# Shift and scale of the dense stage: from VectorE's sums to TensorE's two lines, inside the attention

## The chip, the cores and the metric

The kernel runs on one core of one Trainium2 chip. The metric is device time in microseconds (us), the median of several executions. TensorE is called PE in the profile, VectorE DVE, ScalarE ACT, GpSimd POOL, SyncE SP.

## The reference

Two blocks of two layers each, over 256 tokens of width 1024. The first block has a hybrid mixer (gated linear attention beside a sparse attention with a compressed, a selected and a window branch), a dense feed-forward part, a Mamba-2 mixer and a mixture of experts. Ahead of each of the four stands a modulation that depends on the conditioning vector `c` alone:

```python
def adaln(c, w, b):
    mod = jax.nn.silu(c) @ w + b
    shift, scale, gate = jnp.split(mod[:, None, :], 3, axis=-1)
    return shift, scale, gate

def modulate(x, norm_w, shift, scale):
    return rmsnorm(x, norm_w) * (1 + scale) + shift
```

`w` is 1024 x 3072 in float32, so each of shift (part 0), scale (part 1) and gate (part 2) is a vector of 1024 numbers out of 4 MB of weights. The change is about how shift and scale of the dense stage are computed, and when.

## The kernel before

The stages of the first block follow one another: hybrid input projection with the gated linear attention, the sparse attention, the hybrid output projection with the residual addition and norm, the dense stage, then Mamba and experts. Each engine has its own program, in an order written out by hand; semaphores tie them. Weights of 2 MB a piece come over SyncE's queue into `slots`.

The modulation vectors that are not needed at once are made beside this main work, and called side work here. `SIDE` lists it: the gate of hyb, then dense, ssm and moe, each with its parts. A part is eight chunks `k` of 128 rows by 1024 columns, 512 KB each, loaded by GpSimd into three buffers in turn: `beside[0]`, `beside[1]` and a `gates` buffer. VectorE multiplies chunk `k` by `sc[:, k]` (silu of c, one number a partition) and adds it to the accumulator `macc` (128 x 1024): line 150 for the first chunk, line 153 for the others. After the eighth chunk the sum over the 128 partitions is left, and TensorE makes it. For shift and scale these are eight products with a column of ones (`column_sums`), and `column_done` adds the bias and writes `s2` or `s1` (in the trace `s_dense`, `s_ssm`). For the gate, which is needed on all partitions, they are two products of 128x512 with a matrix of ones, each followed on VectorE by the addition of the bias rows (`gate`); the one side bank of the attention is taken by them in turn. A buffer is loaded again when its accumulation has signalled; `macc` can be started again when the sums are made.

Three generators hold this side work for GpSimd, VectorE and TensorE (`side_gpsimd`, `side_vector`, `side_tensor`). The main programs advance them by one unit wherever `c.side_v.step()` or `c.side_t.step()` stands; `pace = (a, b)` lets through those of every b calls that the test in `step` allows, and `until` runs the side work up to a named point. Only these calls set where a side instruction stands in an engine's order. An instruction whose data are late holds up all that stands behind it on its engine.

In the sparse attention `branch_*` are the selected and the window branch (scores `S<-..`, their transposes by `k_ident`, products `vb,PT`), `compressed_*` makes the compressed keys (`xk`, hidden `hx`, `hy`, `hz`, its transpose `hid`, then `kcT` and `vbd`), and `blocks_*` scores them (`cs`, `cp`, `ct`, `AT`). Its output is `mix`, which the output projection takes.

Of the kernel before, what the change touches and what calls it, by code (L numbers as in the profile page):

```python
# [437 lines left out]
SIDE = (("hyb", 0, 2, (2,)), ("dense", 1, 2, (0, 1, 2)), ("ssm", 2, 2, (0, 1, 2)), ("moe", 0, 0, (0, 1, 2)))  # L438
# [316 lines left out]
def first(c):  # L755
# [105 lines left out]

    def column_done(e, tsig, vsig, name, part):
# [65 lines left out]
    def jobs():  # L928
        for name, slot, third, which in SIDE:
            chunks = [(p, k) for p in which for k in range(KC)]  # L930
            yield name, slot, [beside[:, 0, :], beside[:, 1, :], gates[third][:, :]], chunks

    def side_gpsimd(e, me):

        free = [S.t.at(("cols", now[-1])), NOTHING, S.t.at(("mod", "hyb", 1))]
        for name, slot, bufs, chunks in jobs():
# [4 lines left out]
            def get(n):  # L941
                part, k = chunks[n]
                e.wait_ge(*free[n % 3])
                e.dma_start(bufs[n % 3], w[k * 128:(k + 1) * 128, part * D:(part + 1) * D]).then_inc(*beside_landed[n % 3].up((name, n)))
# [5 lines left out]
            for n, (part, k) in enumerate(chunks):  # L950
# [3 lines left out]
                free[n % 3] = side.v.at((name, n))  # L954
# [13 lines left out]
    def side_vector(e, me):  # L968
        last = NOTHING
        for name, slot, bufs, chunks in jobs():  # L970
            yield
            yield
            for n, (part, k) in enumerate(chunks):
                yield
                e.wait_ge(*beside_landed[n % 3].at((name, n)))
                if k == 0:
                    e.wait_ge(*last)
                    e.tensor_scalar(macc[:, :], bufs[n % 3], sc[:, 0:1], ALU.mult).then_inc(*side.v.up((name, n)))
                else:
                    e.wait_ge(*side.v.at((name, n - 1)))  # L980
                    e.scalar_tensor_tensor(macc[:, :], bufs[n % 3], sc[:, k:k + 1], macc[:, :], ALU.mult, ALU.add).then_inc(*side.v.up((name, n)))
# [4 lines left out]
                yield  # L986
                yield
# [15 lines left out]
    def side_tensor(e, me):  # L1003
        for name, slot, bufs, chunks in jobs():
            yield
            yield
            for n, (part, k) in enumerate(chunks):
                yield
                if k < KC - 1:
                    continue  # L1010
# [3 lines left out]
                yield  # L1014
                if part < 2:
                    column_sums(e, side.t, macc, side.v.at((name, n)), name, part, c.side_banks)
                    me.done.add((name, ("cols", part)))
                    continue
                for i in range(2):
                    ps = c.side_banks.take(("gate", name, i))  # L1020
                    e.wait_ge(*ps.was)
                    e.wait_ge(*side.v.at((name, n)))
# [10 lines left out]
def hybrid(c):  # L1033
# [400 lines left out]
    def compressed_tensor(e):  # L1434
# [13 lines left out]
        c.side_t.step()  # L1448
        for _ in range(3):
            yield  # L1450
# [37 lines left out]
    def compressed_vector(e):  # L1488
# [23 lines left out]
        c.side_v.step()  # L1512
        for _ in range(3):
            yield
# [31 lines left out]
    def blocks_tensor(e, hf):  # L1546
        qs = slice(hf * 128, hf * 128 + 128)
        for gi in range(2):
# [6 lines left out]
            m.then_inc(*t.up(("Sc", hf, gi)))  # L1555
            yield
# [3 lines left out]
        e.transpose(ps.t[:, 0:128], small[hf][4][:, :], K["ident"]).then_inc(*t.up(("pc", hf)))  # L1560
        yield
# [4 lines left out]
        e.matmul(ps.t[:, :], small[hf][5][:, :], vbd[:, :, :].rearrange("p a d -> p (a d)")).then_inc(*t.up(("oc", hf)))  # L1566
        yield
# [10 lines left out]
    def blocks_vector(e, hf):  # L1578
# [3 lines left out]
        for gi in range(2):  # L1582
# [6 lines left out]
            if gi == 0:  # L1589
                yield  # L1590
        mine = v.now()
        yield
# [18 lines left out]
        c.psum.leave(("nsa_pc", hf), v)  # L1611
        yield
# [4 lines left out]
        c.psum.leave(("nsa_oc", hf), v)  # L1617
        yield

    def branch_tensor(e, br):  # L1620
# [3 lines left out]
        for hf in range(2):  # L1624
# [3 lines left out]
            for gi in range(2):  # L1628
                for j0 in range(0, 4, per):
# [4 lines left out]
                    m.then_inc(*t.up(("s", br, hf, gi, j0)))  # L1634
                yield
# [19 lines left out]
            m.then_inc(*t.up(("o", br, hf)))  # L1655
            yield
# [23 lines left out]
    def branch_vector(e, br):  # L1680
# [3 lines left out]
        for hf in range(2):  # L1684
            nk = (hf + 1) * 128
            per = 512 // nk
            for gi in range(2):
# [10 lines left out]
                e.tensor_reduce(mx_[:, gi * 4:gi * 4 + 4], S_[:, gi * 4:gi * 4 + 4, 0:nk], ALU.max, negate=True).then_inc(*v.up(("max", br, hf, gi)))  # L1698
                yield
# [19 lines left out]
            c.psum.leave(("nsa_o", br, hf), v)  # L1719
            yield  # L1720
# [25 lines left out]
    def tensor(e):  # L1746
        c.side_banks = bs
        e.wait_ge(*v.at(("HT", 7)))
# [6 lines left out]
        S.t.mark("in_end")  # L1755
# [2084 lines left out]
```

## Time and profile before

| | |
|---|---|
| time, median of 3 | 2633.59 us (2630.77 to 2640.56) |
| profiled execution | 2639.54 us, its span 2637.7 us |
| busy share of TensorE, VectorE, ScalarE, GpSimd | 92%, 75%, 54%, 8% |
| input projection (45.3 to 156.0) | 110.7 us |
| sparse attention (156.0 to 264.4) | 108.4 us |
| output projection, residual, norm (264.4 to 304.4) | 40.0 us |
| dense stage (304.4 to about 516.8) | 212.4 us |

The stages lie one behind the other, so a stage's time is that of the chain through it. The busy shares are means over stages that are bound in different ways. Times inside the trace are from the start of the span.

### The profile page before, as it was taken

The numbers are of one execution on the slowest core, as the hardware profiler recorded it, in microseconds if no ns is written. First come the engines' busy times: TensorE is split into PE (matmuls) and PEld (weight loads), VectorE is DVE, ScalarE is ACT, GpSimd is POOL, SyncE is SP. The second block draws the span as 40 slices with busy tenths as digits, with TensorE's granted clock in tenths as the row PEclk, the third lists the DMA queues.
The fourth block names the chain that finished last, engine by engine and source line by source line (L and its number), as shares of the span: only waits on it lengthen the run. The fifth ranks groups of instructions, "written<-read, shape, count | busy, mean of one in ns | idle before, by whom it ended". The sixth has DMA issues, their size and how long they took to land.

```text
span 2637.7 us, 32879 instructions
## 1 busy us (share of the span) xinstructions
PE 2425.0 (92%) x13850; PEld 2105.0 (80%) x13850; DVE 1984.6 (75%) x2208; ACT 1431.5 (54%) x1594; POOL 210.9 (8%) x265
## 2 busy tenths in 40 slices
PE   4877899898899999999999999998997999897998
PEld 3756799687777888888888888887886997886997
DVE  6756777686657888989888889886666775767675
ACT  3312443464546777767676767675444653444562
POOL 1101001000000000000000000000311110221110
PEclk8986899897889999999999999999998999998999
DMA  9652678432246999999999999995224453323551
GB/s 317 214 201 88 213 273 297 161 133 92 96 171 231 348 361 347 360 349 359 352 354 345 360 342 365 340 368 186 96 76 151 162 211 136 115 78 118 197 185 76
DMA packets 263559, 608.44 MB, mean 231 GB/s; under 512 B 18472, under 2 KB 33083, under 8 KB 263403
## 3 DMA queue, kind: packets, MB, share of 16 engines
q1 hardware_dynamic: 247808, 554.39, 58.4%
q0 software_dynamic: 14640, 51.49, 5.7%
q8 instruction: 111, 1.82, 0.3%
q10 hardware_dynamic: 954, 0.37, 0.1%
q14 instruction: 46, 0.37, 0.0%
HBM read 605.17 MB, written 1.05 MB: 230 GB/s over the span
## 4 chain that ended last, share of the span: by engine, by line
PE 80%; DVE 10%; ACT 5%; DMA 2%; issue 1%; POOL 1%; SPq 0%; PEldq 0%; PEld 0%; DVEq 0%; ACTq 0%; POOLq 0%
PE ps L132 78%; PE ps L136 2%; DVE eb L153 1%; DMA slots<-in_hyb_mod_w 1%; DVE X L153 1%; ACT L142 1%; DVE ul_in L145 1%; DVE xn L153 1%; DVE macc L153 1%; ACT uh_ffn L139 0%; DMA beside<-in_dense_mod_w 0%; ACT eb L139 0%; ACT xn L139 0%; DVE ul_ssm_w L145 0%; DVE gate L153 0%
## 5 line engine op out<-in xcount | busy, mean ns | idle before, releaser
L145 DVE TENSOR_TENSOR ul_moe_w<-slots,uh_moe_w 128x2048 fp32r<-128x2048 f32 x334 | 762.6, 2290 | 108.4 <-ACT uh_moe_w L139 108.2
L139 ACT ACTIVATE uh_moe_w<-slots 128x2048 fp32r<-128x2048 f32 x334 | 640.1, 1918 | 215.7 <-PE ps L132 188.9
L132 PE MATMUL ps<-uh_moe_w,XGh 128*128 128x512 f32 x896 | 356.6, 398 | 3.1 <-DVE XGl L145 2.1
L132 PE MATMUL ps<-uh_moe_w,XGl 128*128 128x512 f32 x896 | 349.5, 390 | 0.0
L132 PE MATMUL ps<-ul_moe_w,XGh 128*128 128x512 f32 x896 | 348.9, 389 | 0.0
L145 DVE TENSOR_TENSOR ul_ffn<-slots,uh_ffn 128x2048 fp32r<-128x2048 f32 x62 | 142.1, 2292 | 100.7 <-ACT uh_ffn L139 100.7
L132 PE MATMUL ps<-HTf,uh_ffn 128*128 128x256 f32 x704 | 201.2, 286 | 2.8 <-DVE HTlf L145 2.8
L132 PE MATMUL ps<-HTf,ul_ffn 128*128 128x256 f32 x704 | 200.8, 285 | 0.0
L132 PE MATMUL ps<-HTlf,uh_ffn 128*128 128x256 f32 x704 | 200.8, 285 | 0.0
L132 PEld LDWEIGHTS ps<-uh_moe_w,XGh 128*128 128x128 f32 x896 | 168.3, 188 | 38.8 <-DVE XGl L145 2.3
L132 PEld LDWEIGHTS ps<-uh_moe_w,XGl 128*128 128x128 f32 x896 | 168.2, 188 | 35.8
L132 PEld LDWEIGHTS ps<-ul_moe_w,XGh 128*128 128x128 f32 x896 | 168.4, 188 | 35.1 <-issue 1.7
L139 ACT ACTIVATE uh_ffn<-slots 128x2048 fp32r<-128x2048 f32 x66 | 125.7, 1911 | 96.1 <-PE ps L132 96.1
L132 PE MATMUL ps<-uh_moe_w,ehTh 128*128 128x512 f32 x448 | 177.2, 395 | 0.0
L132 PE MATMUL ps<-ul_moe_w,ehTh 128*128 128x512 f32 x448 | 174.6, 390 | 0.0
L132 PEld LDWEIGHTS ps<-HTf,uh_ffn 128*128 128x128 f32 x704 | 137.0, 195 | 3.6 <-DVE HTlf L145 3.6
L132 PE MATMUL ps<-uh_moe_w,ehTl 128*128 128x512 f32 x448 | 138.1, 389 | 0.0
L132 PEld LDWEIGHTS ps<-HTlf,uh_ffn 128*128 128x128 f32 x704 | 136.9, 194 | 0.0
L132 PEld LDWEIGHTS ps<-HTf,ul_ffn 128*128 128x128 f32 x704 | 136.8, 194 | 0.0
L145 DVE TENSOR_TENSOR ul_dense_w<-slots,uh_dense_w 128x2048 fp32r<-128x2048 f32 x33 | 75.5, 2291 | 45.0 <-ACT uh_dense_w L139 45.0
L145 DVE TENSOR_TENSOR ul_ssm_w<-slots,uh_ssm_w 128x1024 fp32r<-128x1024 f32 (+1 forms) x57 | 68.5, 1204 | 54.0 <-ACT uh_ssm_w L139 53.9
L132 PE MATMUL ps<-HTm,uh_in 128*128 128x256 f32 (+1 forms) x336 | 102.5, 305 | 7.2 <-DVE HTlm L145 4.1
(511 smaller groups left out, 5565.0 us busy)
## 6 DMA issues: line engine op xcount, KB each, us to landing
slots<-in_moe_w_gu SPq DMA_DIRECT2D x111, 2048.0 KB, 8.6
slots<-in_moe_w_down SPq DMA_DIRECT2D x56, 2048.0 KB, 8.1
slots<-in_w_up SPq DMA_DIRECT2D x20, 2048.0 KB, 7.9
slots<-in_w_in SPq DMA_DIRECT2D x14, 2048.0 KB, 8.5
slots<-in_dense_w_gu SPq DMA_DIRECT2D x10, 2048.0 KB, 10.1
slots<-in_ssm_w_in SPq DMA_DIRECT2D x10, 2048.0 KB, 8.1
slots<-in_w_down SPq DMA_DIRECT2D x10, 2048.0 KB, 8.4
slots<-in_dense_w_down SPq DMA_DIRECT2D x5, 2048.0 KB, 12.3
```

Of the source, the lines that this page charges most:

```text
L132: return self.e.matmul(o, lhsT, rhs, start=start, stop=stop, skip_group_check=skip) if self.e else DONE
L136: return self.e.transpose(o, i, ident[0:n, 0:n]) if self.e else DONE
L139: return self.e.activation(o, i, f, **kw) if self.e else DONE
L142: return self.e.preload_act_table_set("natural_log_exp_and_others") if self.e else DONE
L145: return self.e.tensor_tensor(o, a, b, op) if self.e else DONE
L153: return self.e.scalar_tensor_tensor(o, a, s, b, op0, op1) if self.e else DONE
```

## The change

Dense part 2 (the gate) is now made first, by VectorE as before. Parts 0 and 1 follow it inside the attention, and TensorE makes them without VectorE's accumulation: for each chunk two products, the column `sc[:, k]` of 128 partitions as weights against each half of the chunk, accumulated over the eight chunks. They end in two lines of 512 numbers, on partitions 0 and 64 of one PSUM bank. VectorE copies the two lines to partition 0 of `macc`, and eight products of one row each turn them into the eight columns that `column_done` expects. A buffer of these two parts is freed by TensorE's products.

With this the steps move: a pace of (3, 5) in the input projection, one of (1, 1) in the attention with more places for steps, and `until` at both ends of the attention. The orders of ScalarE and SyncE stay as they were.

```diff
-SIDE = (("hyb", 0, 2, (2,)), ("dense", 1, 2, (0, 1, 2)), ("ssm", 2, 2, (0, 1, 2)), ("moe", 0, 0, (0, 1, 2)))
+SIDE = (("hyb", 0, 2, (2,)), ("dense", 1, 2, (2,)), ("dense", 1, 2, (0, 1)), ("ssm", 2, 2, (0, 1, 2)), ("moe", 0, 0, (0, 1, 2)))
+LINES = (("dense", (0, 1)),)
...
+    def lines_tensor(e, name, part, k, x, landed):
+
+        if k == 0:
+            ps = c.side_banks.take(("lines", name, part))
+            e.wait_ge(*ps.was)
+        ps = c.psum.of(("lines", name, part))
+        e.wait_ge(*S.v.at("sc"))
+        e.wait_ge(*landed.at((name, part, k)))
+        for i, r in enumerate((0, 64)):
+            m = e.matmul(ps.t[r:r + 1, :], sc[:, k:k + 1], x[:, i * 512:(i + 1) * 512], k == 0, k == KC - 1)
+        m.then_inc(*side.t.up((name, part, k)))
+
+    def lines_to_columns(e, name, part):
+
+        ps = c.side_banks.take(("mod", name, part))
+        e.wait_ge(*ps.was)
+        e.wait_ge(*S.g.at("ones"))
+        e.wait_ge(*side.v.at(("lines", name, part)))
+        for i in range(8):
+            m = e.matmul(ps.t[:, i:i + 1], macc[0:1, i * 128:(i + 1) * 128], ones[0:1, 0:1])
+        m.then_inc(*side.t.up(("mod", name, part)))
...
     def side_gpsimd(e, me):
...
-                free[n % 3] = side.v.at((name, n))
+                free[n % 3] = (side.t if by_lines else side.v).at((name, part, k))
...
     def side_vector(e, me):
...
+                if by_lines:
+                    ps = c.psum.of(("lines", name, part))
+                    e.wait_ge(*side.t.at((name, part, k)))
+                    e.wait_ge(*last)
+                    for i, r in enumerate((0, 64)):
+                        e.tensor_copy(macc[0:1, i * 512:(i + 1) * 512], ps.t[r:r + 1, :]).then_inc(*side.v.up(("lines", name, part)))
+                    c.psum.leave(("lines", name, part), side.v)
...
     def side_tensor(e, me):
...
+                if by_lines:
+                    lines_tensor(e, name, part, k, bufs[n % 3], beside_landed[n % 3])
...
     def tensor(e):
         c.side_banks = bs
+        c.side_t.pace = (3, 5)
...
         S.t.mark("in_end")
+        c.side_t.until(("hyb", "rows"))
+        c.side_t.pace = (1, 1)
         weave(branch_tensor(e, 0), branch_tensor(e, 1), blocks(e, 0, compressed_tensor, blocks_tensor), blocks(e, 1, None, blocks_tensor))
+        c.side_t.until(("dense", ("cols", 1)))
```

VectorE's program (`vector`) gets the same four lines for `c.side_v`. A `step()` is added in the loops of `branch_tensor` and `branch_vector` (behind the scores and behind the products), in `blocks_tensor` and `blocks_vector` (behind each piece), and in the three waiting turns of `compressed_tensor` and `compressed_vector`.

TensorE's order in the middle of the attention, from the last chunk products of part 0 to the scores of the second half. A product is named out<-moving,weights; `hx` is the hidden layer of the compressed keys, `vb,PT` the branches' output products, `kb,nq` the scores:

```order
+L132 MATMUL ps<-beside,sc 1x512 x2
+L136 MATMUL ps<-k_ident,S 128x128 x2
+L132 MATMUL ps<-beside,sc 1x512 x2
 L136 MATMUL ps<-k_ident,hx 128x30 x4
 L132 MATMUL ps<-vb,PT 128x64 x16
+L132 MATMUL ps<-ones,macc 128x1 x8
 L132 MATMUL ps<-hid,w 64x16 x4
-L132 MATMUL ps<-kb,nq 128x256 x8
+L132 MATMUL ps<-kb,nq 128x256 x4
+L132 MATMUL ps<-gate,sc 1x512 x2
+L132 MATMUL ps<-kb,nq 128x256 x4
+L132 MATMUL ps<-beside,sc 1x512 x2
```

The chunk products (1x512) now stand ahead of the transposes of `hx`, and the eight products that make the columns of part 0 ahead of the work with `hid`, all in front of `kb,nq`.

VectorE's order at the same place, from the hidden layer's last operations to the first scores of the second half:

```order
 L145 TENSOR_TENSOR hx<-hx,hz 30x512
-L153 SCALAR_TENSOR_TENSOR macc<-gate,sc,macc 128x1024
-L153 SCALAR_TENSOR_TENSOR macc<-beside,sc,macc 128x1024 x2
-L156 COPY PT<-ps 128x2x128
-L153 SCALAR_TENSOR_TENSOR macc<-gate,sc,macc 128x1024
-L156 COPY PT<-ps 128x2x128
-L153 SCALAR_TENSOR_TENSOR macc<-beside,sc,macc 128x1024 x2
-L153 SCALAR_TENSOR_TENSOR macc<-gate,sc,macc 128x1024
+L156 COPY PT<-ps 128x2x128 x2
 L156 COPY hid<-ps 128x4x15 x2
 L145 TENSOR_TENSOR Og<-ps,fac 128x512
+L156 COPY macc<-ps 1x512 x2
 L145 TENSOR_TENSOR mix<-ps,fac 128x512
+L145 TENSOR_TENSOR s_dense<-ps,v_m 128x8
```

Seven accumulations are gone from between `hx` and `hid`; the copy of the two lines and `s_dense` stand behind `hid`.

VectorE's order at the end of the attention, up to `mix`, where before the copies of PT, `AT`, `Og` and `mix` had three accumulations of ssm among them:

```order
 L153 SCALAR_TENSOR_TENSOR macc<-gate,sc,macc 128x1024
+L156 COPY PT<-ps 128x512
+L153 SCALAR_TENSOR_TENSOR macc<-beside,sc,macc 128x1024
+L145 TENSOR_TENSOR AT<-ps,cf 128x512
+L153 SCALAR_TENSOR_TENSOR macc<-beside,sc,macc 128x1024
+L145 TENSOR_TENSOR AT<-ps,cf 128x512
+L153 SCALAR_TENSOR_TENSOR macc<-gate,sc,macc 128x1024
+L153 SCALAR_TENSOR_TENSOR macc<-beside,sc,macc 128x1024 x2
 L145 TENSOR_TENSOR Og<-ps,fac 128x512
 L145 TENSOR_TENSOR mix<-ps,fac 128x512
+L145 TENSOR_TENSOR s_ssm<-ps,v_m 128x8
 L145 TENSOR_TENSOR mix<-mix,AT 128x512 x2
```

Here accumulations of ssm part 0 have been moved in, and with them its column (`s_ssm`), which stands ahead of the two additions that finish `mix`. On GpSimd the loads of two more chunks (`beside<-in_ssm_mod_w`) stand ahead of the `AT` additions.

## Rows read from the trace of the kernel before

**Rows 1.** The page: span, and TensorE's busy time and share

```profile
span 2637.7 us, 32879 instructions
...
PE 2425.0 (92%) x13850; PEld 2105.0 (80%) x13850; DVE 1984.6 (75%) x2208; ACT 1431.5 (54%) x1594; POOL 210.9 (8%) x265
```

**Rows 2.** Stretches: length, PE, PEld, DVE, ACT, POOL busy, PEclk, DMA, GB/s

```profile
45.30:156.00 110.70, 96.86 (x604) 83.28 (x604) 77.48 (x102) 36.08 (x56) 12.38 (x24) 0.90 0.72 231
156.00:209.30 53.30, 35.24 (x164) 23.73 (x164) 27.56 (x50) 8.70 (x39) 3.69 (x8) 0.73 0.45 157
209.30:240.60 31.30, 27.41 (x96) 21.42 (x96) 18.08 (x55) 9.12 (x34) 2.09 (x4) 0.53 0.17 68
304.40:502.40 198.00, 198.00 (x1376) 185.55 (x1376) 138.18 (x127) 74.87 (x78) 20.05 (x38) 0.99 0.76 267
```

**Rows 3.** Chain of waits, input projection: start us, us, what

```profile
82.18 1.28 DVE macc L153
...
127.17 1.20 DVE macc L153
...
152.81 1.29 DVE macc L153
```

**Rows 4.** Chain of waits, attention

```profile
198.84 3.73 DMA gate<-in_dense_mod_w
...
204.17 3.90 DMA gate<-in_dense_mod_w
...
209.30 0.35 DVE hid L156 x2
...
259.93 0.68 DVE mix L145
```

**Rows 5.** Timeline of TensorE: start us, us, instructions, idle before [releaser]

```profile
128.51 2.85 PE L132 MATMUL ps<-ones,macc 128*128 128x1 f32 x16 [1.17 <-DVE macc L153]
...
185.69 1.84 PE L132 MATMUL ps<-ones,macc 128*128 128x1 f32 x16
...
201.73 7.09 PE L132 MATMUL ps<-vb,PT 128*128 128x64 f32 x32 [3.69 <-DVE PT L156]
...
236.09 1.92 PE L132 MATMUL ps<-macc,ones 128*128 128x512 f32 x2
...
238.78 1.12 PE L132 MATMUL ps<-macc,ones 128*128 128x512 f32 x2 [0.78 <-DVE gate L145]
...
251.36 7.33 PE L132 MATMUL ps<-vb,PT 128*128 128x64 f32 x64 [0.34 <-ACT PT L139]
...
576.97 2.85 PE L132 MATMUL ps<-eb,xt 128*64 128x256 f32 x16 [1.27 <-DVE eb L153]
```

**Rows 6.** Timeline of VectorE

```profile
232.71 0.68 DVE L156 COPY PT<-ps 128x512 f32<-128x512 f32 x1
...
287.03 0.74 DVE L150 TENSOR_SCALAR macc<-gate,sc 128x1024 f32<-128x1024 f32 x1
```

**Rows 7.** Busy time and granted clock (PEclk) in short stretches, columns as above

```profile
128.00:136.00 8.00, 7.49 (x38) 7.52 (x39) 5.72 (x12) 0.00 (x0) 1.06 (x2) 0.58 0.98 330
...
224.00:228.00 4.00, 4.00 (x19) 3.44 (x18) 2.63 (x5) 1.20 (x5) 0.00 (x0) 0.50 0.00 0
...
245.30:248.70 3.40, 2.89 (x11) 2.38 (x12) 2.08 (x7) 0.00 (x0) 0.00 (x0) 0.50 0.00 0
...
249.00:258.00 9.00, 8.66 (x71) 7.80 (x69) 4.87 (x6) 1.08 (x2) 4.13 (x5) 1.00 0.61 178
```

**Rows 8.** DMA issues, 190 to 265: size, median us to landing

```profile
beside<-in_dense_mod_w POOLq DMA_DIRECT2D x3, 512.0 KB, 4.9
beside<-in_ssm_mod_w POOLq DMA_DIRECT2D x4, 512.0 KB, 4.7
```

**Rows 9.** Chain of waits, end of the dense stage

```profile
491.77 7.71 DMA gate<-in_moe_mod_b
...
499.58 1.29 DVE gate L145 x2
```

More of the change, by code:

```diff
@@ L930, in jobs @@
             chunks = [(p, k) for p in which for k in range(KC)]
-            yield name, slot, [beside[:, 0, :], beside[:, 1, :], gates[third][:, :]], chunks
+            yield name, (name, which) in LINES, slot, [beside[:, 0, :], beside[:, 1, :], gates[third][:, :]], chunks
     def side_gpsimd(e, me):
         free = [S.t.at(("cols", now[-1])), NOTHING, S.t.at(("mod", "hyb", 1))]
-        for name, slot, bufs, chunks in jobs():
+        for name, by_lines, slot, bufs, chunks in jobs():
             w = io[name + "_mod_w"][0]
@@ L969, in side_vector @@
         last = NOTHING
-        for name, slot, bufs, chunks in jobs():
+        for name, by_lines, slot, bufs, chunks in jobs():
             yield
@@ L974, in side_vector @@
                 yield
[L975 to L981, printed above, removed]
+                if not by_lines:
+                    e.wait_ge(*beside_landed[n % 3].at((name, part, k)))
+                    if k == 0:
+                        e.wait_ge(*last)
+                        e.tensor_scalar(macc[:, :], bufs[n % 3], sc[:, 0:1], ALU.mult).then_inc(*side.v.up((name, part, k)))
+                    else:
+                        e.wait_ge(*side.v.at((name, part, k - 1)))
+                        e.scalar_tensor_tensor(macc[:, :], bufs[n % 3], sc[:, k:k + 1], macc[:, :], ALU.mult, ALU.add).then_inc(*side.v.up((name, part, k)))
                 if k < KC - 1:
@@ L1003, in side_tensor @@
     def side_tensor(e, me):
-        for name, slot, bufs, chunks in jobs():
+        for name, by_lines, slot, bufs, chunks in jobs():
             yield
@@ L1014, in side_tensor @@
                 yield
+                if by_lines:
+                    lines_to_columns(e, name, part)
+                    me.done.add((name, ("cols", part)))
+                    continue
                 if part < 2:
-                    column_sums(e, side.t, macc, side.v.at((name, n)), name, part, c.side_banks)
+                    column_sums(e, side.t, macc, side.v.at((name, part, k)), name, part, c.side_banks)
                     me.done.add((name, ("cols", part)))
@@ L1555, in blocks_tensor @@
             m.then_inc(*t.up(("Sc", hf, gi)))
+            c.side_t.step()
             yield
@@ L1611, in blocks_vector @@
         c.psum.leave(("nsa_pc", hf), v)
+        c.side_v.step()
         yield
@@ L1617, in blocks_vector @@
         c.psum.leave(("nsa_oc", hf), v)
+        c.side_v.step()
         yield
@@ L1655, in branch_tensor @@
             m.then_inc(*t.up(("o", br, hf)))
+            c.side_t.step()
             yield
@@ L1719, in branch_vector @@
             c.psum.leave(("nsa_o", br, hf), v)
+            c.side_v.step()
             yield
@@ L1789, in vector @@
     def vector(e):
+        c.side_v.pace = (3, 5)
         modulated_vector(c, e, S, "hyb", hT, hTl, 0)
@@ L1803, in vector @@
             gla_vector(e, n)
+        c.side_v.until(("hyb", "rows"))
+        c.side_v.pace = (1, 1)
         c.lead("hyb_in")
@@ L1807, in vector @@
         weave(branch_vector(e, 0), branch_vector(e, 1), blocks(e, 0, compressed_vector, blocks_vector), blocks(e, 1, None, blocks_vector))
+        c.side_v.until(("dense", ("cols", 1)))
         c.lead("hyb_attention")
```

15 lines of the change are left out of this document (11 added, 4 removed).

## The prediction

> **What bounds the kernel now.** I read the page first, then busy time by stretch, then the chain of waits inside the stretches that the change touches, and the timelines of TensorE and VectorE where the chain points. TensorE is busy 92% of 2637.7 us [rows 1], but not evenly [rows 2]. In the dense stage it is busy 198.00 of 198.00 us: VectorE work removed there is worth nothing. In the input projection it is idle 14 of 110.7 us, in the attention's first 84.6 us (156.0 to 240.6) 22. Only there can about twenty microseconds of VectorE work matter, and only where one of its accumulations (macc) lies on the chain.
>
> It does so in few places. In the input projection one macc of 1.28 us stands ahead of Ee at 82.18, one of 1.20 us at 127.17 ahead of the column sums, and one at 152.81 (with a twin behind it) ahead of vb and gt, for which the first attention products wait [rows 3]. In the attention the chain goes through the load of chunks: a landing of 3.73 us at 198.84, another of 3.90 us, then hid at 209.30 [rows 4]. VectorE is not short of time there; it waits for transfers that could start only when an accumulation had freed their buffer. The gate rows (two products of 128x512 with a VectorE addition between them, on one PSUM bank) are a second place, at 236.09 and 238.78 [rows 5]. (A product in fp32 is two records in the trace: x2 there is one product, x16 are eight.)
>
> **The change part by part.** It takes away 16 accumulations of part 0 and 1 of dense (14 of 1.28 us, two of 0.74 us: 19.4 us of VectorE [rows 3, 6]) and the 16 column products over 128 rows. It adds on TensorE 32 products of 1x512, 16 column products from the lines, and on VectorE four copies of 1x512. The loads are the same in number, but two buffers of three are now freed by TensorE, and dense part 2 comes first.
>
> *Input projection.* The pace is slower, so fewer accumulations lie in it. The macc at 82.18 moves behind Ee: -1.2. The column sums at 128.51 go, with the wait ahead of them: TensorE was idle 1.17 us, the eight products took 2.7 to 2.85 [rows 5], and the stretch 128 to 136 ran at a granted clock of 0.58 [rows 7], that is mostly at 1.2 of 2.4 GHz: of the 5 us left in it for the projection's products a bit over 2 are lost: -6.0. One of the two macc at 152.81 goes: -1.3. Together -8.5.
>
> *Attention to the compressed keys.* VectorE now has two macc ahead of the first xk (+2.6) and one more ahead of the second (+1.3); the xk products are waited for. The dense gate rows' products are put ahead of the S transposes: one product and one addition from 236.09 to 238.78 are 2.7, partly beside ACT's work: +1.5. The eight chunk products of part 0 stand ahead of the transposes of hx, in program order. They wait for loads: three chunks lie ready, the other five need two turns of the buffers, each a product, a hand-over, and a landing of 3.73 to 4.9 [rows 4, 8], say 6.5. First products near 191, next near 197.5, last near 204, then transposes: hid near 208.5, where it was 209.30. So the 12 us between hx and hid stay: the accumulations there only covered loads, and products of TensorE wait for the same loads.
>
> Behind hid stands what was hidden. The vb,PT products of 201.73 (x32) ran beside the wait, in 7.09 us; now they follow the chunk products. The same products at 251.36 (x64) took 7.33 [rows 5], at a granted clock of 1.00 [rows 7], so 3.7 at full clock and 7.1 at 1.2 GHz. Then the two copies of the lines (1.3; a copy of 128x512 takes 0.68 [rows 6]) and eight column products (1.84 to 2.85 [rows 5]). All stand ahead of kb,nq: with -0.7 from hid, and less what of it ran behind hid before (some 1.5), the first kb,nq starts 4.6 later at full clock, 8.7 later at 1.2 GHz.
>
> The cost of one pair of chunk products is not in the trace. Lower bound: side by side. At 576.97 eight fp32 products with 64 columns of weights take 2.85 us [rows 5], of which four have 256 columns and four 128; priced one after another from the 1.7 to 1.9 of a product of 512 they would take 5.1: two column halves of the array run together. The pair here goes to PSUM partitions 0 and 64, which are such halves. Then it costs one 512 product: 1.7 to 1.9 at 1.2 GHz and 0.9 to 1.1 at 2.4, as macc,ones took 1.92 at 236.09 and 1.12 at 238.78 [rows 5]. Upper bound: double. I take the lower; the upper is a rival.
> By the Trainium skill (TensorE: Matmul & The Clock Gate, "Part 3: Packing small matmuls"), products whose outputs lie in different column groups of the array run concurrently, with the second starting some ns after the first; the group at 576.97 fits that, and the sum would be the same by it.
>
> *Second half.* The eight pairs of part 1 lie between products that are 64 rows deep and ran at 0.50 (224 to 228 [rows 7]). They add 8 x 1.7 = 13.6 if the clock stays there; at 2.4 GHz they add 6.9, and the kb,nq and kcT products (27.41 busy of 31.3 [rows 2]) take half. The gate rows' turns, 4.3 us from 236.3 to 240.6, are gone. What the clock does decides. The stretch with full-depth products, 249 to 258, ran at 1.00, while the shallow ones stayed at 0.50 even when busy 4.00 of 4.00 [rows 7]. The chunk products are 128 rows deep. I take it that the clock is up for about half of this time: with the +4.6 from before, the compressed softmax starts 1 later than at 240.6.
> The Trainium skill says of transposes that the full clock doesn't engage for them (the same page, "Part 4: PE-mode transpose"); here 245.3 to 248.7, mostly transposes, ran at 0.50, in agreement, and 249 to 258, mostly products, at 1.00 [rows 7]. By that rule part 0's products, spaced by transposes, would not raise the clock and the first rival would follow.
>
> *End of attention.* Seven accumulations of ssm part 0 must end before s_ssm, which stands ahead of the mix additions on VectorE. Chunk 0 at about 243.5, chunk 1 at 246.5, then each buffer turns in 1.28 + 0.3 + 4.7 [rows 8]: chunk 4 at 252.8, chunk 7 at 259.1, ending at 260.4. Og and mix 1.4, beside them the column sums (1.84), s_ssm 0.2, mix additions 1.28: their end near 264.3, against 259.93 + 0.68 = 260.6 [rows 4]: +3.7, with the 1 later included. The AT additions on GpSimd, now behind two more issues of loads, end before the last accumulation and are hidden.
>
> *Output projection.* Ahead of ul_dense_w stood s_ssm and one macc of 0.74 [rows 6]; now two of 1.28, the last one waiting for its load: +1.3 to +3.5, taken +2.5. TensorE's eight column products there are not on the chain at 287.
>
> *Dense stage.* Seven macc fewer in a stage that is all TensorE: 0. But moe's rows come earlier, and at its end the chain waits 7.71 us for the load gate<-in_moe_mod_b, until the gate additions at 499.58 [rows 9], which stand ahead of ul_ssm_w and the residual addition. Without this wait the first token half's chain starts near 497, and the second half's becomes the bound: -3.1 (its X ends at 505.7 and not 508.9).
>
> **Sum.** The attention counts whole, as its +3.7. -8.5 + 3.7 + 2.5 - 3.1 = -5.4. The clock may be less kind; I take -4: 2639.5 becomes 2635.5. The profiled execution of before took 2639.54 (its span 2637.7 and 1.9 around it), 6 above the median of 2633.59; so the median is forecast at 2629.6, rounded to 2630. What a measurement of this kernel can tell from no change is about 0.5%, 13 us.
>
> **Rivals.**
> 1. *The clock stays at 1.2 GHz through the second half* (slower side). The lines make the half longer without raising the clock: +8.7 at its start, 13.6 for the pairs, 1.84 to 2.85 for the columns, less 4.3 for the gate rows, less what the pairs find as idle time (31.3 - 27.41 = 3.9): about +14 to +18 at 240.6. With -8.5, +2.5, -3.1 and +2.7 (the 3.7 without its 1): +8 to +12 net, 2641 to 2645. For it: 224 to 228 at 0.50 while busy [rows 7]; against: the deep products. It decides from the moment when the kb,nq stretch is at 0.50 with the pairs in it.
> 2. *The two products of a pair run one after another.* 16 pairs each 0.86 to 1.7 more; in part 0 the loads hide them, in part 1 they don't: +7 to +14, time 2637 to 2643; with rival 1, 2650. Against: 576.97 [rows 5].
> 3. *The gain is larger.* The loads land in 3.7, as at 198.84 [rows 4], in every turn, and the clock is up in all of the second half: hid 3 us earlier, second half 5 shorter, the wait at the end of attention 3 shorter: -15 to -16: 2618. For it: one row of 3.73 and one of 3.90; against: the medians of 4.7 to 4.9 [rows 8].
> 4. *Nothing changes*, since all of it stands in stretches bounded by loads: the chunks' 512 KB loads are as many. Then input projection's -8.5 is given back by the attention: 2632 to 2636.
> By the Trainium skill (DMA: Bandwidth & Descriptors, "Anatomy of one DMA"), a load of 512 KB would take about 2.0 + 1.2 = 3.2 us; no landing here is so short (3.73 at 198.84), and the sum uses the rows.
>
> **Chances and range.** Forecast 0.40, rival 1 0.17, rival 2 0.10, rival 3 0.18, rival 4 0.15. Faster by over 0.5% (below 2620.4): most of rival 3 and a tail of the forecast, 0.20. Slower by over 0.5% (above 2646.8): rivals 1 and 2 together, or a late load at the end of attention twice over, 0.10. Within: 0.70. The range is 2616 to 2645: below, two thirds of rival 3, above, rival 1 and the lower end of 2. The forecast's own is 2622 to 2637.
>
> **What would show it.** Right: no column products near 128 and the clock near 1.00 from 128 to 136; the input projection 8 shorter; hid still near 12 us after hx with TensorE waiting for loads of in_dense_mod_w; a pair lasting as long as one 512 product; mix additions 3 to 4 later relative to the stage's start; no wait for in_moe_mod_b. Wrong: the stretch kb,nq to kcT at 0.50 with the pairs in it (rival 1), pairs of double length (rival 2), hid much earlier (rival 3). The step I trust least is the clock in the second half.

## The result and the profile after

The changed kernel takes 2646.03 us (median of 18 runs, 2639.47 to 2654.86), the kernel before 2636.81 (18 runs, 2628.79 to 2646.9). The ratio is 1.0029, with a 95% interval of 1.0017 to 1.0041: 7.6 us slower (4.5 to 10.8), where 4 us less were forecast. It lies just above the forecast range (2645) and on the other side of no change, though within the 0.5% bound. The forecast counted from the median of 2633.59 that before had in its first three executions; by the ratio, the same change on that base is 2641.2.

The page of the changed kernel, its span and TensorE's line, to be set beside [rows 1]: TensorE is busy 16 us longer, VectorE 15 less.

```profile
span 2649.7 us, 32981 instructions
...
PE 2441.2 (92%) x13914; PEld 2098.1 (79%) x13914; DVE 1969.2 (74%) x2196; ACT 1431.7 (54%) x1594; POOL 211.9 (8%) x265
```

Busy time and granted clock by stretch (length, PE, PEld, DVE, ACT, POOL, PEclk, DMA share, GB/s): the input projection, the attention up to the end of the vb,PT products, from there to the compressed softmax, to the output projection, and the dense stage. They answer to [rows 2].

```profile
44.00:146.50 102.50, 90.30 (x587) 76.95 (x587) 65.86 (x92) 38.23 (x61) 6.52 (x13) 0.97 0.64 202
146.50:204.40 57.90, 41.04 (x184) 19.28 (x184) 24.85 (x50) 8.82 (x39) 7.41 (x15) 0.82 0.60 200
204.40:247.30 42.90, 41.37 (x152) 22.88 (x153) 18.26 (x54) 8.30 (x32) 4.21 (x8) 0.60 0.28 89
247.30:276.50 29.20, 16.99 (x115) 14.43 (x112) 23.00 (x41) 6.55 (x12) 6.72 (x10) 0.73 0.50 158
317.60:515.20 197.60, 197.60 (x1376) 185.15 (x1376) 132.49 (x123) 76.74 (x82) 16.34 (x31) 0.99 0.72 258
...
218.50:232.00 13.50, 13.47 (x35) 7.52 (x35) 6.36 (x12) 4.95 (x21) 1.36 (x3) 0.50 0.26 78
```

The third row is the one to look at: TensorE is busy 41.37 of 42.90 us there, at a granted clock of 0.60. In the kernel before, the stretch from 209.3 to 240.6 had 27.41 us in it. The last row is a part of it, busy 13.47 of 13.50 us at 0.50.

TensorE's timeline in the attention (a chunk's pair of products is x4, four records). It answers to [rows 5].

```profile
180.01 1.02 PE L132 MATMUL ps<-macc,ones 128*128 128x512 f32 x2
...
185.07 1.03 PE L132 MATMUL ps<-beside,sc 128*1 128x512 f32 x4 [0.34 <-DVE gate L145]
...
193.02 1.87 PE L132 MATMUL ps<-beside,sc 128*1 128x512 f32 x4 [1.22 <-DMA beside<-in_dense_mod_w]
...
199.05 1.03 PE L132 MATMUL ps<-beside,sc 128*1 128x512 f32 x4 [0.96 <-DMA beside<-in_dense_mod_w]
...
200.36 3.79 PE L132 MATMUL ps<-vb,PT 128*128 128x64 f32 x32
...
204.45 1.94 PE L132 MATMUL ps<-ones,macc 1*128 1x1 f32 x16 [0.30 <-DVE macc L156]
...
206.87 3.78 PE L132 MATMUL ps<-kb,nq 64*128 64x256 f32 x8
210.58 1.87 PE L132 MATMUL ps<-gate,sc 128*1 128x512 f32 x4
...
236.03 1.87 PE L132 MATMUL ps<-beside,sc 128*1 128x512 f32 x4
...
238.88 1.77 PE L132 MATMUL ps<-gate,sc 128*1 128x512 f32 x4
...
241.18 1.03 PE L132 MATMUL ps<-beside,sc 128*1 128x512 f32 x4
...
245.01 1.94 PE L132 MATMUL ps<-ones,macc 1*128 1x1 f32 x16 [0.92 <-DVE macc L156]
```

A pair takes 1.03 us at 2.4 GHz and 1.87 at 1.2. Part 0's pairs (185 to 200) run at the high clock, but for the one behind a wait for a load at 193.02 and part of the next, and vb,PT needs 3.79, the full-clock price. From 204.45 on (one-row products, then 64-row products kb,nq) the groups run at 1.2 GHz until about 240.6: part 1's first pair at 210.58 and six more take their 1.87 or near it, and only the last is at full clock. Part 1's own column products stand at 245.01, ahead of cm.

VectorE's timeline: the end of hx and hid, the copies of part 1's lines, s_dense and the first operation of the compressed softmax (cm), the last accumulation of ssm in the attention, s_ssm and the mix additions.

```profile
191.94 0.68 DVE L145 TENSOR_TENSOR hx<-hx,hz 30x512 f32<-30x512 f32 x1
...
200.41 0.35 DVE L156 COPY hid<-ps 128x60 f32<-128x60 f32 x2 [7.13 <-PE ps L136]
...
243.56 1.39 DVE L156 COPY macc<-ps 1x512 f32<-1x512 f32 x2
...
246.99 0.17 DVE L145 TENSOR_TENSOR s_dense<-ps,v_m 128x8 f32<-128x8 f32 x1 [1.59 <-PE ps L132]
...
247.27 0.28 DVE L159 TENSOR_REDUCE cm<-cs 128x8 f32<-128x128 f32 x1
...
266.90 1.28 DVE L153 SCALAR_TENSOR_TENSOR macc<-beside,sc,macc 128x1024 f32<-128x1024 f32 x1 [0.71 <-DMA beside<-in_ssm_mod_w]
...
270.28 0.17 DVE L145 TENSOR_TENSOR s_ssm<-ps,v_m 128x8 f32<-128x8 f32 x1 [0.90 <-PE ps L132]
...
270.41 2.35 DVE L145 TENSOR_TENSOR mix<-mix,AT 128x512 f32<-128x512 f32 x2
```

The end of hx in the kernel before, from the same view:

```profile
196.68 0.68 DVE L145 TENSOR_TENSOR hx<-hx,hz 30x512 f32<-30x512 f32 x1
```

The chain of waits at the attention's end, against [rows 4]: two landings of ssm chunks between accumulations, and 1.64 us ahead of the second mix addition for which the profile names no releaser.

```profile
256.56 3.79 DMA beside<-in_ssm_mod_w
...
261.96 4.92 DMA beside<-in_ssm_mod_w
...
270.44 1.64 issue
```

GpSimd's timeline suggests what it is: two loads are issued at 266.49 and 268.48, and the AT additions that mix needs come behind them.

```profile
268.48 0.53 POOL L177 DMA_DIRECT2D beside<-in_ssm_mod_w  x1 [1.46 <-DVE macc L153]
269.10 2.50 POOL L145 TENSOR_TENSOR AT<-AT,Og 128x512 f32<-128x512 f32 x2
```

Set against the kernel before, with the forecast (in its own terms, cumulative), the changed kernel stands so (us; minus is earlier):

| point | before | after | difference | forecast |
|---|---|---|---|---|
| first kb,nq (input projection done) | 155.99 | 146.52 | -9.5 | -8.5 |
| first xk product | 161.97 | 154.39 | -7.6 | -5.9 |
| hid | 209.30 | 200.41 | -8.9 | -9.2 |
| first kb,nq of the second half | 210.34 | 206.87 | -3.5 | -3.9 |
| compressed softmax (cm) | 240.55 | 247.27 | +6.7 | -7.5 |
| first output projection product | 264.8 | 276.9 | +12.1 | -4.8 |
| first dense product | 304.4 | 317.6 | +13.2 | -2.3 |
| first Mamba product | 516.7 | 526.5 | +9.8 | -5.4 |
| span | 2637.7 | 2649.7 | +12.0 | -4 |

The forecast held up to the second half of the attention, and for the dense stage; it was 14 us wrong between the first kb,nq of the second half and cm. The last 2.2 us of the span's +12.0 are probably not the change's: behind the Mamba stage (from its first product with yTh, 729.7 in before, 738.2 here) the trace of before needs 1908.0 us to its end, and every other trace of this document, that of the padded kernel before too, 1910.8 or more.

### The profile page after: what moved, and what is told of

It is laid out like the page before. It is cut to its first block, busy times and chain, and to the rows that moved or that the text cites. A ratio compares the mean times of both kernels' runs of the same rounds, so it can differ in the third digit from the quotient of the medians.

```text
span 2649.7 us, 32981 instructions
## 1 busy us (share of the span) xinstructions
PE 2441.2 (92%) x13914; PEld 2098.1 (79%) x13914; DVE 1969.2 (74%) x2196; ACT 1431.7 (54%) x1594; POOL 211.9 (8%) x265
## 4 chain that ended last, share of the span: by engine, by line
PE 81%; DVE 10%; ACT 5%; DMA 2%; issue 1%; POOL 1%; SPq 0%; PEldq 0%; PEld 0%; DVEq 0%; ACTq 0%; POOLq 0%
PE ps L132 79%; PE ps L136 2%; DVE eb L153 1%; DMA slots<-in_hyb_mod_w 1%; DVE X L153 1%; ACT L142 1%; DVE ul_in L145 1%; DVE xn L153 1%; ACT uh_ffn L139 0%; DVE macc L153 0%; DMA beside<-in_ssm_mod_w 0%; ACT eb L139 0%; DVE gate L153 0%; DVE gcv L153 0%; ACT xn L139 0%
```

## The experiments

Two theories stood at first. A: in the second half TensorE is the bound, at 1.2 GHz, and part 1's pairs cost their full price. B: the loss is in the order of the steps, the accumulations of ssm and the late s_ssm at the attention's end above all. All ratios are to the kernel before on the same chip.

### Without lines

```diff
-LINES = (("dense", (0, 1)),)
+LINES = ()
```

> The changed kernel's order and pace, but both parts are made by VectorE's accumulations and TensorE's column sums over 128 rows, as before; no line products. Theory A (the pairs of part 1 run at 1.2 GHz in the second half of the attention and lie wholly on TensorE's path, 14.4 us, with the two copies and eight one-row products behind them): the time from the first kb,nq to the compressed softmax falls from some 40 to some 30 us, and the kernel by 8 to 12, to about the kernel before. Theory B (the loss is in the order of the steps: accumulations of ssm and a late s_ssm at the attention's end, whoever makes the dense parts): the time stays within 3 us of the changed kernel, about 1.003 of before.

Measured: 2643.67 us, ratio 1.0030 (1.0012 to 1.0047), the same as with lines. Neither number of theory A came; theory B's, 1.003, did. The Mamba stage starts 9.7 us later than before, as in the changed kernel (9.8), by other ways: hid is at 207.0 and not 200.4, since VectorE's accumulations stand in front of it, and the second half (first kb,nq to cm) takes 34.5 us in place of 40.4. Its row:

```profile
211.30:245.80 34.50, 26.44 (x97) 22.66 (x96) 24.31 (x58) 8.31 (x32) 4.21 (x8) 0.50 0.33 97
```

and two groups of TensorE's timeline in it, the column sums of parts 0 and 1, each behind a wait for the last accumulation:

```profile
207.23 3.54 PE L132 MATMUL ps<-ones,macc 128*128 128x1 f32 x16 [3.42 <-DVE macc L153]
...
241.92 3.54 PE L132 MATMUL ps<-ones,macc 128*128 128x1 f32 x16 [3.52 <-DVE macc L153]
```

So the lines gain 6.6 us up to hid and have lost them again at the output projection. Theory B isn't shown by its number: the second half is longer than before without lines too (34.5 against 30.2), with eight accumulations that VectorE now makes between its scores. Two costs of other kinds come out alike here.

### Lines for part 0 alone

```diff
-SIDE = (("hyb", 0, 2, (2,)), ("dense", 1, 2, (2,)), ("dense", 1, 2, (0, 1)), ...
-LINES = (("dense", (0, 1)),)
+SIDE = (("hyb", 0, 2, (2,)), ("dense", 1, 2, (2,)), ("dense", 1, 2, (0,)), ("dense", 1, 2, (1,)), ...
+LINES = (("dense", (0,)),)
```

> Lines for part 0 alone, in the first half, where TensorE waits for loads; part 1 by VectorE's accumulations in the second half, where VectorE has room. Theory A: the second half loses its 8 pairs, 14.4 us less TensorE work, of which some 10 show; the first half stays as in the changed kernel (first kb,nq near 207); in all 8 to 14 us below the changed kernel, ratio to before 0.997 to 1.000. Theory B: no more than 3 us below the changed kernel. A third possibility: the eight accumulations now delay VectorE's scores and copies in the second half, and what TensorE gains is lost there; then the stretch is as long but TensorE idle in it.

Measured: 2657.04 us, ratio 1.0075 (1.0053 to 1.0098): slower than both. The first half is as expected (first kb,nq at 206.5). From there to cm it takes 36.9 us, the third possibility:

```profile
206.50:243.40 36.90, 28.01 (x102) 23.83 (x100) 24.50 (x57) 9.49 (x34) 4.21 (x8) 0.50 0.33 98
```

```profile
239.58 3.55 PE L132 MATMUL ps<-ones,macc 128*128 128x1 f32 x16 [5.62 <-DVE macc L153]
```

TensorE is idle 9 of 36.9 us, 5.62 of them ahead of the column sums. The Mamba stage starts 7.7 us later than before, 2 earlier than in the changed kernel, but the trace ends 15.1 later than that of before: 7 come in stages whose code is the same (below, on what isn't settled).

### No side step from the end of dense's parts to the output projection

```diff
     def step(self):
+        if self.hold in self.done:
+            return
         self.calls += 1
...
+        c.side_t.hold = ("dense", ("cols", 1))
         weave(branch_tensor(e, 0), branch_tensor(e, 1), ...)
         c.side_t.until(("dense", ("cols", 1)))
+        c.side_t.hold = None
```

(the same for VectorE's steps).

> The changed kernel, but once part 1 is done no side step is taken before the output projection, so that no accumulation of ssm lies in the attention and s_ssm and the AT additions are where they were. Theory A: the attention's end, 5 us longer than before after the compressed softmax, is as before, and the end of the dense stage waits for the moe gate bias again (3 us): in all 2 to 5 below the changed kernel, ratio 1.001 to 1.002. Theory B: the whole loss goes, 9 to 12 below.

Measured: 2662.69 us, ratio 1.0098 (1.0077 to 1.012). The dense stage starts at +8.2 in place of +13.2, the 5 us of theory A, though 1.5 of them stand already at cm (245.78), ahead of what the hold changes, so about 3.5 are the hold's. But they are more than lost at the end of the dense stage, where the chain goes through a load of moe's last part and its accumulation, ahead of the residual addition:

```profile
501.97 7.60 DMA beside<-in_moe_mod_w
...
509.60 1.28 DVE macc L153
```

The Mamba stage starts at +17.8. The side work has a due time at both ends: what it doesn't do in the attention stalls the end of the dense stage.

With part 1 by accumulations, the same hold, and a step at every place of the dense stage (pace (1, 1) for (4, 5)):

> Both: part 1 by VectorE, no side step between the end of dense and the output projection, and one step at every place of the dense stage in place of four of five, so that moe's rows still come in time there. Theory A: the two savings add up, 13 to 18 below the changed kernel, 0.996 to 0.998 of before. Theory B: as e3 within 3 us.

Measured: 2659.04 us, ratio 1.0084 (1.0063 to 1.0105). The dense stage starts at +4.3, the earliest so far, and loses it inside: steps that come faster than loads land (8.30 us in this row of its chain) hold up VectorE's splits and so TensorE.

```profile
436.73 8.30 DMA beside<-in_moe_mod_w
```

### Stop after the fourth chunk of ssm

As the hold above, but the steps stop only once the fourth ssm chunk is accumulated:

```diff
-        c.side_t.hold = ("dense", ("cols", 1))
+        c.side_t.hold = ("ssm", 0, 4)
...
             for n, (part, k) in enumerate(chunks):
                 yield
+                if k:
+                    me.done.add((name, part, k - 1))
```

> The changed kernel, but the side steps stop in the attention after the fourth chunk of ssm and go on in the output projection. From the runs so far the attention's end costs 5 us because seven accumulations and s_ssm stand ahead of mix, and stopping altogether gave those 5 back but came too late for moe at the end of the dense stage. Expected: the dense stage starts 3 to 5 us earlier than in the changed kernel, and moe is still in time, so 3 to 5 below it, ratio 1.001 to 1.002. Rival: the side work is late in the dense stage already with four chunks less, and the gain is lost there: no change or slower than the changed kernel.

Measured: 2656.24 us, ratio 1.0084 (1.0063 to 1.0104). No gain, as the rival said, but not by its mechanism: the dense stage starts at +15.8, 2.6 later than in the changed kernel and not earlier, since cm is already 2.4 later (249.71), and the dense stage itself takes 210.5 against 209.0. Mamba starts at +13.9. The hold acts only behind cm, so this difference of 2.4 us ahead of it is not the edit's work; single traces differ by so much.

### Pairs of part 1 made twice

```diff
         for i, r in enumerate((0, 64)):
             m = e.matmul(ps.t[r:r + 1, :], sc[:, k:k + 1], x[:, i * 512:(i + 1) * 512], k == 0, ...)
+        if part == 1:
+            for i, r in enumerate((0, 64)):
+                m = e.matmul(ps.t[r:r + 1, :], sc[:, k:k + 1], x[:, i * 512:(i + 1) * 512], False, k == KC - 1)
```

> The changed kernel with each pair of products of part 1 made twice (the shift or scale of that part comes out doubled); nothing else moves. Theory A, as it stands after the runs without lines (in the second half of the attention TensorE is the bound at 1.2 GHz and a pair costs its full 1.87 us): the time from the first kb,nq to the compressed softmax grows by 8 x 1.87 = 15 us and the kernel by 13 to 16 over the changed one, about 1.008 of before. Theory C (the pairs fill time in which TensorE would wait for VectorE or for loads): under 6 us.

Measured: 2638.14 us, ratio 1.0020 (1.0002 to 1.0039). Twice the products, and the kernel isn't slower than the changed one but, by the medians' ratios, 2 us faster, if anything; the second half takes 35.3 us in place of 40.4. Neither number came. The row shows why, and the timeline with it (x8 are four products now, two pairs):

```profile
207.50:242.80 35.30, 33.83 (x160) 17.20 (x159) 17.33 (x51) 8.30 (x32) 4.21 (x8) 0.89 0.37 117
```

```profile
211.17 2.89 PE L132 MATMUL ps<-gate,sc 128*1 128x512 f32 x8
...
215.91 1.88 PE L132 MATMUL ps<-beside,sc 128*1 128x512 f32 x8
...
229.22 1.06 PE L132 MATMUL ps<-kcT,nq 64*128 64x16 f32 x8
...
230.21 1.88 PE L132 MATMUL ps<-beside,sc 128*1 128x512 f32 x8
```

The granted clock is 0.89. The first double pair at 211.17 still takes 2.89; from 215.91 on two pairs take 1.88, what one took before, and kcT,nq x8 1.06 in place of 1.89. So the cost of part 1 isn't mainly the products' work. It is that TensorE stays at its lower level. The same 64-row scores ran at either level: x8 of kb,nq takes 3.78 at 207.46 and 1.99 at 213.99.

### Pairs of part 1 cut to 8 columns

```diff
+            n = 512 if part == 0 or k == 0 else 8
-            m = e.matmul(ps.t[r:r + 1, :], sc[:, k:k + 1], x[:, i * 512:(i + 1) * 512], ...)
+            m = e.matmul(ps.t[r:r + 1, 0:n], sc[:, k:k + 1], x[:, i * 512:i * 512 + n], ...)
```

> The changed kernel with the products of part 1 cut to 8 columns of 512 from the second chunk on (the rest of that part's sum is left out); waits, loads and order stay. Theory A: the second half loses about 7 x 1.8 = 12.6 us of TensorE work and 9 to 12 us of time, so the kernel falls to within 3 us of before or under it. Theory C: under 4 us, as the waits for loads appear instead.

Measured: 2639.03 us, ratio 1.0009 (0.9990 to 1.0028), within 3 us of before as theory A said. The second half gives less than it asked: it takes 34.8 us at a clock of 0.50, 5.6 less than with whole pairs, not 9 to 12.

```profile
206.30:241.10 34.80, 31.96 (x128) 24.00 (x127) 17.30 (x52) 8.30 (x32) 4.23 (x8) 0.50 0.37 121
```

Cutting part 1's products to about an eighth and doubling them bring nearly the same: less work at 1.2 GHz, or more of it at 2.4.

### Scores at full depth

The score products contract over 64 partitions, one head group. Here they go over all 128:

```diff
-qT[gi * 64:gi * 64 + 64, j, qs], kb[br][gi * 64:gi * 64 + 64, 0:nk]
+qT[:, j, qs], kb[br][:, 0:nk]
...
-qT[gi * 64:gi * 64 + 64, j, qs], kcT[gi * 64:gi * 64 + 64, :]
+qT[:, j, qs], kcT[:, :]
```

> The changed kernel with the score products kb,nq and kcT,nq over all 128 partitions in place of the 64 of one head group (the scores are then sums over both groups, other numbers than the reference's); as many products of the same columns. Theory A with the clock as the cause: the 64-row products hold the granted clock at 0.50, and full-depth ones let it rise as xk does: the stretch from the first kb,nq to the compressed softmax goes from 0.50 to 0.57 to above 0.9, pairs from 1.87 to 1.03 us, and 12 to 18 us go, to 0.996 or so of before. Rival: the clock does not depend on their depth and the time stays.

Measured: 2633.60 us, ratio 0.9989 (0.9975 to 1.0003), 10 us below the changed kernel. Products of the same number and the same columns; the clock goes to 0.83 and the stretch to 30.9 us. That is 9.5 less, where 12 to 18 were expected:

```profile
209.00:239.90 30.90, 27.83 (x130) 16.70 (x129) 17.24 (x51) 8.30 (x32) 4.22 (x8) 0.83 0.42 136
```

### Padded keys, in three kernels

The same depth with the reference's scores: for each head group a copy of the keys in which the other group's rows are zero, used in the second half, and kcT likewise in both halves. It takes the room of two buffers that are free by then.

```diff
+    kz = [za, cum]
...
+        for j in range(2):
+            e.memset(kz[j][:, :, :].rearrange("p a b -> p (a b)"), 0.0).then_inc(*g.up(("kz0", j)))
...
+                    e.activation(kz[br][rows, gi, :], kb[br][rows, :], AF.Copy).then_inc(*a.up(("kz", br)))
...
+                        if hf:
+                            m = e.matmul(..., qT[:, j, qs], kz[br][:, gi, :])
```

In the changed kernel:

> The changed kernel with the keys of the second half (kb, and kcT in both halves) padded to 128 partitions: the other head group's rows are zero, so that the scores are the reference's and the products full depth; four small copies on ScalarE, two memsets of 128x512 and one of 128x32 on GpSimd more. Theory A with the clock as the cause: as with the deep scores, the second half runs mostly at 1.00, and 8 to 12 us go against the changed kernel: ratio to before 0.998 to 1.001. Rival (the deep scores gained by something else, such as other values): within 3 us of the changed kernel.

Measured: 2632.73 us, ratio 0.9974 (0.9958 to 0.9990): 6.9 us faster than before (2.6 to 11) and some 16 below the changed kernel, faster than both. From the first kb,nq to cm it takes 28.5 us at 0.92, and cm is at 235.96, 4.6 earlier than before. The late end of the attention stays: the dense stage starts at +1.3 and Mamba at -2.6, so the trace accounts for 2.6 of the 6.9:

```profile
207.40:236.00 28.60, 25.44 (x130) 15.51 (x129) 17.51 (x53) 8.30 (x32) 4.21 (x8) 0.92 0.45 142
```

Two groups of its timeline (the padded keys have the names of the reused buffers, za and cum): scores in 1.99 where they took 3.78, a pair in 1.03.

```profile
211.76 1.99 PE L132 MATMUL ps<-cum,nq 128*128 128x256 f32 x8
...
213.68 1.03 PE L132 MATMUL ps<-beside,sc 128*1 128x512 f32 x4
```

In the kernel before:

> The same padding in the kernel before. Its second half has no pairs, 27.4 us of TensorE work at 0.53 in 31.3. Theory A: the clock rises there too, the work becomes some 15 to 18 us and VectorE's 18 us and the waits between them become the bound: 5 to 9 us less, ratio 0.9965 to 0.998. Rival: without the long fp32 products of 512 columns the score products leave too many gaps, the clock stays at 0.50 and nothing changes.

Measured: 2637.35 us, ratio 0.9990 (0.9971 to 1.0009). The clock goes from 0.53 to 0.68 only, and cm is 1.5 us earlier. This lies between the theory and its rival, nearer the rival. The medians of the two padded kernels are 4.6 us apart, but their intervals overlap; in the traces, Mamba starts at -2.6 with lines and at -0.9 here.

```profile
211.20:239.10 27.90, 23.36 (x90) 17.83 (x88) 16.98 (x51) 8.90 (x33) 1.42 (x3) 0.68 0.23 76
```

In the order without lines:

> The changed kernel's order without lines (as in the first experiment), with the padding. If the clock is what made the line products dear, lines must now be cheaper than accumulations, where at 1.2 GHz both were alike: this kernel stays 3 to 8 us above the padded one with lines. Rival: lines and accumulations are alike at either clock, and both are within 3 us.

Measured: 2642.25 us, ratio 1.0017 (0.9998 to 1.0036), 11 us above the padded kernel with lines by the ratios. Its clock is 0.65, and TensorE is busy 23.12 of 34.4 us: it waits for VectorE's accumulations.

```profile
212.40:246.80 34.40, 23.12 (x99) 20.17 (x98) 24.45 (x59) 8.31 (x32) 4.21 (x8) 0.65 0.33 99
```

So what makes the lines pay is both together: deep scores, and the pairs that stand between them. One alone (0.60 with the pairs, 0.65 and 0.68 with deep scores) leaves the clock low; only the doubled pairs lifted it by themselves, to 0.89.

### The changed kernel again

> The changed kernel once more, for a second trace and more runs beside the same kernel before. The stretches up to the start of the Mamba stage should repeat within 1 us (9.8 later there than before), with the second half of the attention again at 0.50 to 0.62. The Mamba stage, whose code is the same everywhere and which took 201 to 216 us in the traces so far, may come out anywhere in that range; if it repeats 211 it depends on the kernel and not on the execution.

Measured: 2648.34 us, ratio 1.0034 (1.0013 to 1.0054). The second half repeats, 40.1 us at 0.59; the Mamba stage starts at +7.6, so single traces of one kernel differ by 2 us there, more than the 1 expected.

```profile
205.20:245.30 40.10, 38.62 (x128) 20.45 (x127) 17.38 (x51) 8.31 (x32) 4.23 (x8) 0.59 0.30 94
```

## Why the prediction was wrong, point by point

**Input projection, -8.5.** Measured -9.5. The column sums, the wait ahead of them, and the macc ahead of Ee are gone from the chain as forecast; from 44 to 146.5 the granted clock is 0.97, where it was 0.90 [rows 2].

**Attention up to the second half.** Right in its sum. Against the stage's start xk is late by 1.9 (forecast 2.6), hid is where the loads let it be (-8.9 against -9.2), vb,PT takes 3.79 (3.7), the copies and column products stand ahead of kb,nq, which starts at -3.5 (-3.9). But hid came there by another split: "So the 12 us between hx and hid stay" is wrong. They were 12.6 (196.68 to 209.30) and are 8.5 (191.94 to 200.41), as hx itself has moved up by 4.7 and hid by 8.9. TensorE does wait there for loads of in_dense_mod_w (1.76, 1.22 and 0.96 us ahead of pairs), which keeps a part of what the 7 accumulations left. Without lines the same gap is 14.8 (192.19 to 207.00).

**A pair costs one product of 512 columns.** Right: 1.03 and 1.87 us for both products together. Rival 2 is out.

**"I take it that the clock is up for about half of this time: ... the compressed softmax starts 1 later than at 240.6."** This is the step that failed. The range of its price was in the text (13.6 for the pairs at 1.2 GHz, 6.9 at 2.4), and the choice between them rested on the pairs' depth alone. Measured: 0.60 over the stretch, in its middle 0.50; 40.4 us from kb,nq to cm, where 26.6 were forecast and 30.2 stood before. That the clock is the main cause is shown by three runs that raise it from different sides: twice the pairs is 5 us shorter (0.89), the same number of score products at full depth 9 to 12 shorter (0.83 and 0.92). Pairs cut to about an eighth are only 5.6 shorter, at 0.50.

The clock is not all of the 14 us. The padded kernel, with the clock at 0.92, takes 28.5 us, still 1.9 over a forecast that had the clock up for half of the time only. A term that the forecast put at nothing, without a reason, is part 1's own way from lines to columns: the two copies (1.39), the column products (1.94 at 245.01) and s_dense stand ahead of cm. From 243.64, the end of a cs operation, to cm at 247.27 are 3.6 us, of which another cs operation would need 0.41: an estimate of some 3 us from these rows. Rival 1's sum had the column products.

**End of attention, 2.7 beyond the softmax's delay.** Measured 5.4: the last accumulation ends at 268.2, as two chunks are waited for in the chain. The AT additions on GpSimd, which I called hidden, seem not to be: by GpSimd's row they end about 271.6, and the second mix addition starts at 272.08, 1.7 us after the first one; the profile doesn't name the wait. The mechanism was right, the size short by half.

**Output projection, +2.5.** +1.1. **Dense stage, -3.1.** -3.4: no wait for the moe bias any more.

**Rival 1** is what happened, at the place and by the mechanism it named, and its price of 8 to 12 us net is near the 7.6 measured (4.5 to 10.8). At cm it had +14 to +18 against the stage's start, and 16.2 were measured. That the sum fits so well is in part luck: vb,PT ran at the high clock, so kb,nq starts 6.0 later and not 8.7, and the half is longer by 10.2, which is more than its terms behind kb,nq add up to (13.6 - 4.3 - 3.9, and 1.84 to 2.85 if the columns are part 1's: 7 to 8). It had a chance of 17 in 100. Nothing in the trace of before spoke for the clock's rise but the deep products around 249; two rows spoke against, 224 to 228 at 0.50 with TensorE busy all the time [rows 7] and the whole of 209.3 to 240.6 at 0.53 [rows 2], both with the same 64-row products. The range ended at 2645; on the base from which it was counted the measured change is 2641.2, inside it, but on the slower side, where less time was forecast.

The Trainium skill (TensorE: Matmul & The Clock Gate, "Part 4: PE-mode transpose") was weighed for part 0, where its rule would have kept the clock down. The trace doesn't bear that out: pairs spaced by transposes ran in 1.03 us, and four records of transposes between them in 0.60, where they take 1.12 at 1.2 GHz.

**What isn't settled.** The Mamba stage, the same code in all kernels, took 201 to 216 us in the traces (211 in both of the changed kernel, 212 in that of before, 201 without lines), with granted clocks that differ in stretches where TensorE waits often: from 75 to 90 us into the stage TensorE was busy 13.4 us of 15 in both, at 0.66 in the changed kernel and at 0.89 without lines. The runs of one kernel spread over up to 18 us (without lines from 2638 to 2656). Whether the stage's time goes with the execution or with the kernel is open: it repeated in the two traces of the changed kernel, and no other kernel has two. The kernels with the hold or with part 1 by VectorE are slower by 8 to 12 us than the start of their Mamba stage says, and no run tells why. Verdicts here rest on the ratios, and mechanisms on the traces up to that stage, one trace a kernel. What sets the clock's level isn't settled either: depth, the products between the scores and the waits all moved it, and no run took the waits alone.

## What to carry to other kernels

Where TensorE's clock is at its lower level in the stretch that a change fills, price the added products at that level until something in the change is known to raise it, and give this case the main chance. Ask whether an idle-looking engine can be given side work by looking at what sets the end there: the work taken off VectorE had in part only covered loads, and TensorE then waited for the same loads. Price also the tail of the new way (here copies, column products and the row that ends them), wherever it stands ahead of the chain. And a stretch whose shallow products keep the clock low may be mended by padding them to full depth: here this turned a change of +0.3% into one of -0.3%, while the same padding in the kernel before gave -0.1%, not clear of no change.

## What the runs showed of the hardware

More work can take less time: with the pairs doubled, the second half went from 40.4 to 35.3 us, the clock from 0.60 to 0.89. Score products over 64 partitions, back to back with deep products between them (41.37 busy of 42.90 us), stayed mostly at 1.2 GHz; the same count and columns over 128 partitions, half of the rows zero, ran mostly at 2.4 (0.92 over 28.6 us). Full depth is not a condition for the higher level: between doubled pairs the 64-partition scores took 1.99 us for four products, as the padded ones did, and 3.78 at 1.2 GHz. Without the pairs between them even the padded ones reached only 0.65 to 0.68. Two fp32 products of 512 columns whose outputs are single lines at PSUM partitions 0 and 64 take together what one takes, 1.03 us at 2.4 GHz.
